# Hybrid mixer layer on one core: low halves of streamed tiles made by VectorE or loaded, the state mixer's and the sample's steps placed anew, weights loaded late in a pass

## What is computed

```python
h = rms_norm(x, norm_g)
fq, fk, fv, fg, ff, su, sg, mq, mg = split_columns(h @ w_in)
fq = rms_norm(fq per head); fk = rms_norm(fk per head)
logf = log_sigmoid(ff + b_forget)
fox_out = fox_attend(fq, fk, fv, logf) * silu(fg)
ssm_y, h_re, h_im = s5_mixer(su, ...); ssm_out = ssm_y * silu(sg)
mem_out = memory_attention(rms_norm(mq per head), mem_k, mem_v) * silu(mg)
y = x + concat(fox_out, ssm_out, mem_out) @ w_out
```

## Time and profile before

| | |
|---|---|
| median of 3 runs | 1640.53 us (1638.3 to 1640.94) |
| profiled execution | 1635.89 us, span 1634.2 us |
| TensorE matmul busy over the span | 1473.9 us (90%) |
| VectorE, ScalarE, GpSimd busy | 852.7, 713.2, 462.7 us |
| mean granted TensorE clock | 0.966 of full |
| HBM read and written | 167.0 and 75.0 MB |

### The profile page before, as it was taken

How to read it: one execution, slowest core, us unless ns; L and a number is a source line. 1 busy time by engine, 2 the same in 40 slices (tenths; PEclk the granted TensorE clock), 3 DMA queues, 4 the chain that set the end, 5 groups by cost and what they waited for, 6 DMA issues and landing times. The chain is left out here.

```text
span 1634.2 us, 28959 instructions
## 1 busy us (share of the span) xinstructions
PE 1473.9 (90%) x10318; PEld 1209.6 (74%) x10318; DVE 852.7 (52%) x1757; ACT 713.2 (44%) x1726; POOL 462.7 (28%) x491
## 2 busy tenths in 40 slices
PE   7998988988986987998998999999999999599998
PEld 7997756767864766776776778778778777478887
DVE  2578533792443674445443666666666666332221
ACT  5655322321432362444433666666666666311010
POOL 4455655441363674444332000000000000011110
PEclk9999998998998998999998999999999999899999
DMA  6653897471277477676765762461551600335452
GB/s 192 207 170 107 278 247 175 116 238 61 78 178 251 153 219 240 222 238 192 233 199 123 194 137 57 81 137 21 117 108 30 137 2 21 109 113 182 159 178 100
DMA packets 200246, 245.03 MB, mean 150 GB/s; under 512 B 72560, under 2 KB 146704, under 8 KB 196496
## 3 DMA queue, kind: packets, MB, share of 16 engines
q1 hardware_dynamic: 199072, 243.28, 52.5%
q10 hardware_dynamic: 1040, 0.00, 0.0%
HBM read 167.00 MB, written 74.99 MB: 148 GB/s over the span
## 5 line engine op out<-in xcount | busy, mean ns | idle before, releaser
L875 PE MATMUL in_g<-in_wh,in_xs 128*128 128x512 f32 (+2 forms) x1808 | 557.5, 387 | 23.3 <-DVE in_wl L1443 9.5
L875 PEld LDWEIGHTS in_g<-in_wh,in_xs 128*128 128x128 f32 x1808 | 331.3, 194 | 97.3 <-issue 30.9
L875 PE MATMUL in_g<-in_wl,in_xs 128*128 128x512 f32 (+2 forms) x904 | 328.4, 376 | 0.0
L1725 POOL TENSOR_TENSOR in_xs<-in_xu,in_xs 128x512 fp32r<-128x512 f32 x174 | 234.9, 1371 | 315.3 <-ACT in_xs L1161 315.2
L2137 DVE TENSOR_REDUCE attn_tops<-attn_s 128x1 f32<-128x512 f32 (+3 forms) x288 | 171.9, 617 | 144.8 <-PE attn_s L2031 142.8
L2089 ACT ACTIVATE attn_probs<-attn_s,attn_negmax 128x512 f32<-128x512 f32 (+3 forms) x384 | 224.2, 600 | 30.1 <-DVE attn_negmax L2141 29.5
L2044 PE MATMUL attn_t<-all_ident,attn_probs 128*128 128x128 f32 x1216 | 191.3, 276 | 28.2 <-ACT attn_probs_turned L2099 16.3
L2259 POOL TENSOR_TENSOR out_mix<-out_fox 128x512 f32<-128x512 f32 x17 | 22.7, 1336 | 681.8 <-DMA out_ssm<-scratch_ssm 681.8
L1161 ACT ACTIVATE in_xs<-in_xu 128x512 fp32r<-128x512 f32 x174 | 100.1, 623 | 239.2 <-PE in_g L875 193.3
L2044 PEld LDWEIGHTS attn_t<-all_ident,attn_probs 128*128 128x128 f32 x1216 | 143.9, 141 | 70.6 <-issue 30.2
L875 PEld LDWEIGHTS in_g<-in_wl,in_xs 128*128 128x128 f32 x904 | 169.6, 193 | 29.2
(11 more groups left out here) (264 smaller groups left out, 2349.9 us busy)
## 6 DMA issues: line engine op xcount, KB each, us to landing
in_xu<-scratch_xt SPq DMA_DIRECT2D x87, 512.0 KB, 5.0
in_raw<-in_w_in SPq DMA_DIRECT2D x40, 256.0 KB, 5.3
scratch_xt<-in_xu SPq DMA_DIRECT2D x19, 512.0 KB, 5.2
scratch_k<-in_x_turned SPq DMA_DIRECT2D x17, 512.0 KB, 3.9
scratch_q<-in_x_turned SPq DMA_DIRECT2D x17, 512.0 KB, 3.5
in_x_turned<-in_x_prompt SPq DMA_DIRECT2D x16, 512.0 KB, 4.4
in_late<-in_cache_fox_k SPq DMA_DIRECT2D x32, 256.0 KB, 3.8
in_late<-in_cache_fox_v SPq DMA_DIRECT2D x8, 1024.0 KB, 6.9
```

The costliest lines, as they stand in the source:

```text
L875: last = X.matmul(g_ps[b][:, 0:m], xs[:, halves_of(j), h, c, :], ws[:, c, w0:w0 + m], start=(c == 0 and h == 0 and ws is wh), stop=(c == K ...
L1725: G.tensor_tensor(xs[:, halves_of(j), 1, 4 * h:4 * h + 4, :], xu[:, j % 3, 4 * h:4 * h + 4, :], fl(xs[:, halves_of(j), 0, 4 * h:4 * h + 4, ...
```

## The change

- Buffers. `xs` (two high and low pairs) becomes `xh` (two high halves) and `xl` (three low halves); `xu` goes from three buffers to two. The room is the same.
- Low halves. In `state` VectorE makes them in place of GpSimd, and SyncE stores them in HBM next to the whole tile. In `keys`, `queries`, `memkv` and `memq` (`SPLIT`) VectorE makes them. In `values` and `gate` a new step `low_in` loads them two visits ahead. ScalarE makes the high halves as before. GpSimd makes none.
- Order. `split` moves behind `first` of the visit before; `turned_in` moves from part 0 to part 1, and waits for the split of the tile two before (and in `SPLIT` passes for its low half).
- Weights are loaded in visits 7 to 14 of a pass instead of 1 to 8 (`LOADED`).
- S5: the memset of `toep` becomes four, 7 to 13 slots later; the outputs' stores are spread over every second slot and the gate's return goes behind them; `s5_y_in` stands 5 slots later, and the gated product 8 slots later, at four steps in three slots.
- Sample: the steps start a visit earlier; fill and first loads keep clear of the rest, memory queries and values load in a second step, the transposes come 3 slots later within the pattern, so that the eight sequences stay where they were.

```diff
+SPLIT = ("keys", "queries", "memkv", "memq")
+LOADED = 7
...
-            if part == 0 and j + 1 < len(items) and items[j + 1][0] != "state":
-                order.append(("split", j + 1))
-            if part == 0 and j + 3 < len(items):
+            if part == 0 and v + 2 < len(visits):
+                order.append(("low_in", v + 2))
+            if part == 1 and j + 3 < len(items):
                 order.append(("turned_in", j + 3))
...
-            if p not in ("memkv", PASSES[-1]) and part == 2 and 1 <= n_of[v] <= KC:
-                order.append(("weights_in", PASSES.index(p) + 1, n_of[v] - 1))
+            if p not in ("memkv", PASSES[-1]) and part == 2 and LOADED <= n_of[v] < LOADED + KC:
+                order.append(("weights_in", PASSES.index(p) + 1, n_of[v] - LOADED))
             if v and part < 2:
                 order.append((("first", "second")[part], v - 1))
+            if part == 0 and j + 1 < len(items) and items[j + 1][0] != "state":
+                order.append(("split", j + 1))
...
-    main.put(at + 1, "s5_toep_zero")
+    for n in range(4):
+        main.put(at + 8 + 2 * n, "s5_toep_zero", n)
...
-    for n in range(5):
-        main.put(at + n, "s5_y_out", n)
-    main.put(at + 7, "s5_y_in", 0)
-    main.put(at + 9, "s5_y_in", 1)
-    at += 14
+    for n in range(4):
+        main.put(at + 2 * n, "s5_y_out", n)
+    main.put(at + 12, "s5_y_in", 0)
+    main.put(at + 14, "s5_y_in", 1)
+    main.put(at + 8, "s5_y_out", 4)
+    at += 22
...
-    s.put(start, "smp_fill")
-    s.put(start + 1, "smp_in")
-    s.put(start + 4, "smp_turn", 0)
+    s.put(start - 3, "smp_fill")
+    s.put(start - 2, "smp_in", 0)
+    s.put(start + 6, "smp_in", 1)
+    s.put(start + 7, "smp_turn", 0)
...
-    behind += [(pass_start["memkv" if n < 6 else "memq"] + (0 if n < 6 else 2), s) for n, s in enumerate(late.listed())]
+    behind += [(pass_start["memkv" if n < 6 else "memq"] + (0 if n < 6 else 1), s) for n, s in enumerate(late.listed())]
...
+                if what == "low_in" and n[0] >= TILES and visits[n[0]][0] not in SPLIT:
+                    v = n[0]
+                    t = visits[v][1]
+                    sp.wait_ge(s_g, v - 2)
+                    first = next(w for w in range(TILES) if visits[w][1] == t)
+                    sp.wait_ge(s_lst[first % 3], 16 * (first // 3 + 1))
+                    sp.dma_start(fl(xl[:, v % 3, :, :]), D.xt[t, 1]).then_inc(s_lld[v % 3], 16)
...
+                if what == "split" and items[n[0]][0] in SPLIT:
+                    j = n[0]
+                    v = item_visit[j]
+                    dve.wait_ge(s_g, v - 2)
+                    if v - 3 < TILES:
+                        dve.wait_ge(s_lst[v % 3], 16 * ((v - 3) // 3 + 1))
+                    for h in range(2):
+                        dve.wait_ge(s_split_hi, 2 * (j - NX) + h + 1)
+                        V.tensor_tensor(xl[:, v % 3, 4 * h:4 * h + 4, :], xu[:, j % 2, 4 * h:4 * h + 4, :],
+                                        fl(xh[:, v % 2, 4 * h:4 * h + 4, :]), ALU.subtract).then_inc(s_split_lo, 1)
```

More of the change, by code:

```diff
@@ L401, in split_upto, with low_loads, low_made @@
         return sum(1 for p, _, product in items[:max(j + 1, 0)] if p == "state" and product)
-    def halves_of(j):
-        return item_visit[j] % 2
     def turned_loads(j):
-        return sum(1 for i in range(NX, j + 1) if i % 3 == j % 3)
+        return sum(1 for i in range(NX, j + 1) if i % 2 == j % 2)
+    def low_loads(v):
+        return sum(1 for w in range(TILES, v + 1) if w % 3 == v % 3 and visits[w][0] not in SPLIT)
+    def low_made(j):
+        return sum(1 for p, _, _ in items[NX:max(j + 1, NX)] if p in SPLIT)
     def natural(v):
@@ L500, in before_attention @@
         s_split_hi, s_split_lo = a.sem("split_hi"), a.sem("split_lo")
-        s_xst, s_xld = [a.sem(f"xst{i}") for i in range(3)], [a.sem(f"xld{i}") for i in range(3)]
+        s_xst, s_xld = [a.sem(f"xst{i}") for i in range(2)], [a.sem(f"xld{i}") for i in range(2)]
+        s_lst, s_lld = [a.sem(f"lst{i}") for i in range(3)], [a.sem(f"lld{i}") for i in range(3)]
         s_w = [a.sem(f"w{c}") for c in range(KC)]
@@ L718, in _ @@
                     sp.wait_ge(s_kdone, 1)
[L719 removed]
+                    sp.wait_ge(s_zeroed, 4)
                     for s in (2 * n[0], 2 * n[0] + 1):
@@ L782, in decay_in @@
                     sp.dma_start(dec[0:FOX_HEADS, :], D.decay_s[b, :, :]).then_inc(s_dload, 16)
-                if what == "smp_in":
+                if what == "smp_in" and n[0] == 0:
                     s5_done(sp)
@@ L793, in _ @@
                         keys_in(0, f)
+                if what == "smp_in" and n[0] == 1:
                     sp.wait_ge(s_out[pass_start["memq"] % 2], 16 * stored_upto(pass_start["memq"], pass_start["memq"] % 2))
@@ L1444, in _ @@
                                                fl(wh[:, c, 0:m]), ALU.mult, ALU.subtract).then_inc(s_wl, 1)
+                if what == "x":
+                    j = n[0]
+                    if items[j][2] and item_visit[j] >= 3:
+                        v = item_visit[j]
+                        dve.wait_ge(s_g, v - 2)
+                        dve.wait_ge(s_lst[v % 3], 16 * (v // 3))
+                    for h in range(2 if items[j][2] else 0):
+                        v = item_visit[j]
+                        dve.wait_ge(s_xth, 2 * v + h + 1)
+                        dve.wait_ge(s_xu, 2 * j + h + 1)
+                        V.tensor_tensor(xl[:, v % 3, 4 * h:4 * h + 4, :], xu[:, j % 2, 4 * h:4 * h + 4, :],
+                                        fl(xh[:, v % 2, 4 * h:4 * h + 4, :]), ALU.subtract).then_inc(s_xtl, 1)
+                if what == "split" and items[n[0]][0] in SPLIT:
+                    j = n[0]
+                    v = item_visit[j]
+                    dve.wait_ge(s_g, v - 2)
+                    if v - 3 < TILES:
+                        dve.wait_ge(s_lst[v % 3], 16 * ((v - 3) // 3 + 1))
+                    for h in range(2):
+                        dve.wait_ge(s_split_hi, 2 * (j - NX) + h + 1)
+                        V.tensor_tensor(xl[:, v % 3, 4 * h:4 * h + 4, :], xu[:, j % 2, 4 * h:4 * h + 4, :],
+                                        fl(xh[:, v % 2, 4 * h:4 * h + 4, :]), ALU.subtract).then_inc(s_split_lo, 1)
                 if what == "first":
@@ L1718, in _ @@
                     G.tensor_scalar(half[:, t:t + 1], rstd[:, t:t + 1], 0.5, None, ALU.mult).then_inc(s_rstd, 1)
-                if what == "split":
-                    j = n[0]
-                    if order.index(("split", j)) > order.index(("early_fill",)):
-                        pool.wait_ge(K.s_early_fill, 1)
-                    for h in range(2):
-                        pool.wait_ge(s_split_hi, 2 * (j - NX) + h + 1)
-                        G.tensor_tensor(xs[:, halves_of(j), 1, 4 * h:4 * h + 4, :], xu[:, j % 3, 4 * h:4 * h + 4, :],
-                                        fl(xs[:, halves_of(j), 0, 4 * h:4 * h + 4, :]), ALU.subtract).then_inc(s_split_lo, 1)
                 if what == "first" and visits[n[0]][0] in HEADS:
@@ L1739, in _ @@
                 if what == "s5_toep_zero":
+                    k = n[0]
                     pool.wait_ge(s_sg, 16)
-                    G.memset(toep, 0.0).then_inc(s_zeroed, 1)
+                    G.memset(toep[:, GROUPS // 4 * k:GROUPS // 4 * (k + 1), :], 0.0).then_inc(s_zeroed, 1)
                 if what == "decay_in":
@@ L1754, in _ @@
                     pool.wait_ge(s_sel, 4)
-                    pool.wait_ge(s_split_lo, 2 * sum(1 for x in order[:order.index(("early_fill",))] if x[0] == "split"))
                     qb = fl(K.first_head[2][:, :])
```

74 lines of the change are left out of this document (39 added, 35 removed).

## The result

| | before | after |
|---|---|---|
| median | 1639.41 us (1638.16 to 1640.94, 4 runs) | 1571.74 us (1568.92 to 1573.6, 4 runs) |
| profiled execution | 1635.89 us, span 1634.2 | 1571.17 us, span 1569.5 |
| mean granted TensorE clock | 0.966 | 0.982 |

The ratio is 0.9585, 95% interval 0.9567 to 0.9603: 67.7 us faster by the medians. Predicted were 1589 us with a range of 1566 to 1617. The sign was right, and the mechanism in the main; the gain was 27 to 33% larger than the 51 us of the sum (64.7 us between the profiled spans, 67.7 by the medians). Two terms were won by another of the edits than the one that the prediction put first, the scale chain's and the kernel matrices'.

The account below looks back on a forecast made before the run. It took TensorE, busy 90% of the span, as the bound. Gains of 56.5 less costs of 5.5 us, net 51, gave 1584.9 from 1635.89; with 4.6 us for the median, 1589 us was predicted, range 1566 to 1617.

Parts of the forecast that it names:

- scale chain: TensorE's waits for `in_stage`, 10.9 us in 9 waits: two thirds go, with two slow stretches, 10 us gained (bounds 2 and 14).
- kernel matrices: TensorE's wait at L941, 6.6 us in 2 waits: it goes, with 1.5 of clock, 7.5 us gained (bounds 4 and 8.5).
- Low halves on VectorE: VectorE's 140 new subtractions at 0.69 us, mostly covered by its idle time: +2 us cost at pass edges (bounds -3 and +7).
- The scan (L965): TensorE's wait for the end of VectorE's scan goes, with its slow stretch: 12.5 us gained (bounds 4 and 12.5).
- Toep: Wait at L956 for eight pairs of small-row DMAs, with weight chunks now among them: +1.5 us cost (bounds 0 and 7.5).
- Gated product: Wait of 15.2 us at L1002, ended by the second `s5_y_in`: 14 us gained, 2 us of wait left (bounds 8 and 16).
- Sample's start: Waits of 4.0 and 3.9 us at L1035 and L1050: both go, with two slow stretches, 10.5 us gained (bounds 6 and 13).
- Streams and DMA: Tile loads' waits net 0 (bounds -5 and +12); added transfers in gate, values and state cost +2 us (bounds 0 and 15).
- Rivals: 3: VectorE in the scan is held by something that stays, not by GpSimd: 1607 us, chance 0.07.
- 2 by the gate window: Added 512 KB transfers in gate, values and state lengthen a full DMA queue: 1612 us, chance 0.10.
- 4 by the landing times: Slower: with SyncE's single queue and two `xu` buffers, loads land later than TensorE's visit: 1653 to 1695 us, chance 0.05.
- Rival 1: Waits move on to toep's DMAs, the scan or the weight splits; half the gains stay: 1617 us, chance 0.16.

Follow-up runs that it names:

- e8: Kernel before with all 208 low-half subtractions on VectorE instead of GpSimd, old order, no low halves loaded: 1615.24 us, ratio 0.9865.
- e1: Changed kernel with the low halves of the values pass made by GpSimd instead of loaded: 1586.4 us, ratio 0.969.
- e11: Changed kernel with four idle subtractions on GpSimd, which read SBUF, added to each visit of the values pass: 1580.72 us, ratio 0.9658.
- e2: Changed kernel with the low halves of the values pass made by VectorE instead of loaded: 1579.86 us, ratio 0.966.
- e7: Changed kernel with `split` put before `first` again: 1579.95 us, ratio 0.9651.
- e5: Changed kernel with low halves of state, keys, queries, memkv and memq back on GpSimd, values and gate still loaded, new order: 1587.28 us, ratio 0.9693.
- e3: Changed kernel with weights loaded in visits 1 to 8 of a pass again: 1578.31 us, ratio 0.9645.
- e9: Changed kernel with the mixer's drives three slots later and a pause of 20 slots, not 22, before the gated product: 1566.95 us, ratio 0.957.
- e12: Changed kernel with the mixer's drives three slots later and a pause of 21 slots, not 22, before the gated product: 1566.47 us, ratio 0.9563.
- e4: Changed kernel with the mixer's stores, loads back, gated product and final stores in the slots of before: 1578.27 us, ratio 0.9646.
- e6: Changed kernel with the sample's steps in the slots of before, both halves of the first loads together: 1575.48 us, ratio 0.9621.

## Why the prediction was right, and where its sizes were off

**Low halves on VectorE: right.** The 0.69 us are 0.689. My +2 us for the pass edges did not come: the waits for `in_wl` fell from 9.5 to 5.8 us, and e8, which only moves the subtractions, gives the same (5.9): next to no GpSimd subtraction the weight splits are 12% cheaper (854 to 749 ns in the mean). VectorE's busy time, forecast at 910 to 930, is 880: contention had held more of it than I reckoned. POOL busy near 230 was a slip: I took off the 174 subtractions and forgot the 34 of state, which the sum for VectorE did count; it is 197.9.

**The scan (L965), 12.5 us: right,** 10.8 to 0, and GpSimd is the cause (e8, e1, e11). In the values pass the helper's products with the scan's sums took VectorE 54.0 us before and 38.3 after: 15.7 us back, where I had 14. The stretch behind the wait was 0.9 us in e11_reading, where I took 1.7.

**The values pass was mis-sized, the largest miss.** It won 18.7 us, of which the sum had only the scan's 12.5. The group of the product's matmuls in this pass before (295 to 432 us) shows what I left standing:

```profile
L875 PE MATMUL in_g<-in_wh,in_xs 128*128 128x512 f32 x271 | 89.9, 409 | 3.3 <-ACT in_xs L1161 2.3 <-DVE in_wl L1443 1.0
```

With 0.8 for `in_stage` that is 4.1 us of short waits, of which 0.8 are left after. From the first turned weight to the next pass's, TensorE's busy time fell by 4.6 us for 650 matmuls each time, 2.9 more than the 1.7 in the term: 12.5 + 3.3 + 2.9 are the 18.7. That values needs no low half made at all was in the prediction a remark, not a term; e2 shows it worth 12.3 us of pass.

**Scale chain, 10 us: right in size, with the wrong edit first.** `in_stage` went from 10.9 to 4.0, the two thirds that were forecast. The prediction put it down first to `in_hr` no longer standing behind GpSimd's low halves and mentioned the order second. The runs turn that round: without GpSimd's subtractions but in the old order it is 10.2 (e8) or 12.6 (e7), with them but in the new order 5.5 (e5), with both edits 4.0. By the rule that the prediction takes from the Trainium skill, SBUF — State Buffer, "Who interferes with whom", the total would be 3 us less; the chain's three instructions did get slower beside VectorE's subtractions, and TensorE's wait did not show it.

**in_z, 2 us:** 9.5 to 5.6, 3.9 us.

**Kernel matrices, 7.5 us: partly.** Not gone but 6.6 to 2.8 in three waits of up to 1.4. Of the causes listed, GpSimd's low halves were not one: 6.7 us without them in e8, 1.1 with them in e5. With `split` first it is 5.0 (e7), with the weights early 4.0 (e3); the memset was not tried alone.

**Toep, +1.5 us: right,** 7.2 to 7.9; the eight row DMAs keep VectorE's read waiting 14.3 us, and with that it is the longest wait left in the first stage. e9 and e12 cover it.

**Gated product, 14 us: right.** 15.2 to none for the DMA; e4 returns 10.5 of it by the slots alone.

**Sample's start, 10.5 us: right within its bounds.** 7.9 us of waits became 2.6 at L1085; e6 prices the steps at 6 us. Where the rest of the 11.0 us that memkv and memq won comes from stays open: e8, which takes GpSimd's subtractions away, wins 0.9 us there, and of the 6.2 us that e5 loses there 5.3 are waits for the low halves, which GpSimd makes in it.

**Streams and DMA, 0 and +2 us: right.** Landing 5.5 and 4.8 us; `in_xh` 4.8 and `in_xl` 1.3 us against 4.3 before. The shares of 0.74, 0.66 and 0.82 in state, values and gate were forecast at 0.8, 0.6 and 0.8; the gate window, with 17 loads more, went from 137 to 136 us.

**The clock** is the term that was too small as a whole. The sum had some 10 us for slow stretches; the windows' busy time fell by 15.3. The idle time fell by 49.6 us, where the sum had some 46.5 of waits less 5.5 of costs. So of the 14 us beyond the forecast (64.7 us between the two profiled spans against 51) some 5 are clock, and 8 to 9 are waits: costs that didn't come and short waits that I had let stand (`in_wl`, `in_z`). Which waits had cost the clock in keys, queries and memq was not measured one by one. In keys it came to 0.96, under the 0.97 that was forecast.

Rivals: 3 falls by e8, 2 by the gate window, 4 by the landing times. Rival 1, the waits moving on, is seen only at L991, 0.7 us. The parts undone one by one cost 17 (e5), 17 or 10 (values, e1 or e2), 10 (e7), 9 (e3), 9 (e4) and 6 us (e6) by the medians, together 61 to 68 us; by the single profiled spans they are 46 to 54. That is most of the 64.7, and doesn't show whether they overlap.

## What to carry to other kernels

Before counting what an engine's work costs, ask whom it slows: GpSimd's 280 us of reading subtractions held VectorE's two-input instructions up by tens of microseconds, and handing them to the busier engine was a gain of 22 us. A stall of TensorE of 5.8 us cost its length and about 1 us of slow clock; families of short waits, which are easily left out of a sum, were worth as much as one long one. Where one engine both serves a chain and makes material for the next tile, put the chain first in its queue.
